# Expert gates formed from fp32r matmuls of 256 columns a token, in 64 blocks of four tokens

## The reference, cut to what matters

```
s1 = einsum('thd,kd->thk', q[..., :half], keys1);  v1, i1 = top_k(s1, 16)
s2 = einsum('thd,kd->thk', q[..., half:], keys2);  v2, i2 = top_k(s2, 16)
expert = i1 * 128 + i2          # of the 16 best of the 16x16 sums
gate   = softmax(top_s)
z   = einsum('cd,ced->ce', xc, u[expert])
act = gelu(z) * gate
y   = einsum('ce,ced->cd', act, v[expert])
```

## Time and profile before

| | |
|---|---|
| median of three timed runs | 2793.49 us |
| the profiled execution | 2792.25 us, span 2790.4 us |
| PE busy | 2752.2 us (99%) |
| PEld busy | 2406.8 us (86%) |
| DVE busy | 1807.2 us (65%) |
| ACT busy | 1391.5 us (50%) |
| POOL busy | 281.9 us (10%) |
| HBM read | 501.49 MB, 184 GB/s over the span |

### The profile page before, as it was taken

The page is one execution under the profiler, slowest core; times in us unless marked ns, Lnnn a source line. Parts: engine busy times, 40 slices in busy tenths (PEclk is TensorE's granted clock), DMA queues, the critical chain, the costliest instruction groups (busy, mean ns, idle before and its releaser), DMA issues.

```text
span 2790.4 us, 49534 instructions
## 1 busy us (share of the span) xinstructions
PE 2752.2 (99%) x15456; PEld 2406.8 (86%) x15456; DVE 1807.2 (65%) x2899; ACT 1391.5 (50%) x2037; POOL 281.9 (10%) x390
## 2 busy tenths in 40 slices
PE   8999999999999999999999999999999999999998
PEld 6888878888888888889998999888888888888887
DVE  6666665658986666478886666666665555555555
ACT  5454545556665444455555554555454444444444
POOL 0000000000001110000005996000000000000000
PEclk9999999999999999999999999999999999999999
DMA  6544445564555444555565444666666555555564
GB/s 250 188 152 165 156 162 188 180 214 163 173 174 162 155 156 143 193 186 184 186 211 165 156 160 158 217 212 211 213 207 195 193 192 194 193 192 194 192 236 159
DMA packets 153554, 514.76 MB, mean 184 GB/s; under 512 B 17056, under 2 KB 33696, under 8 KB 152480
## 3 DMA queue, kind: packets, MB, share of 16 engines
q1 hardware_dynamic: 131904, 480.44, 52.1%
q10 hardware_dynamic: 21600, 33.70, 3.4%
HBM read 501.49 MB, written 12.58 MB: 184 GB/s over the span
## 4 chain that ended last, share of the span: by engine, by line
PE 86%; issue 10%; DVE 2%; POOL 1%; ACT 1%; DMA 1%; POOLq 0%; DVEq 0%; ACTq 0%; SPq 0%
PE bank L504 21%; PE bank L509 11%; PE bank L2215 8%; PE bank L2217 8%; PE bank L2216 8%; PE bank L542 4%; PE bank L543 4%; PE bank L544 4%; PE bank L489 4%; PE bank L490 4%; PE bank L491 4%; PE bank L2190 2%; DVE w_lo L466 1%; DMA raw<-in_stream 1%; POOL big L623 0%
## 5 line engine op out<-in xcount | busy, mean ns | idle before, releaser
L466 DVE TENSOR_TENSOR w_lo<-raw,w_hi 128x1024 fp32r<-128x1024 f32 x904 | 1096.6, 1224 | 800.8 <-ACT w_hi L457 795.4
L457 ACT ACTIVATE w_hi<-raw 128x1024 fp32r<-128x1024 f32 x904 | 953.2, 1059 | 982.1 <-PE bank L2217 370.1
L504 PE MATMUL bank<-act,w_hi 128*128 128x512 f32 x3072 | 787.0, 398 | 1.1 <-DVE big L1261 1.1
L504 PEld LDWEIGHTS bank<-act,w_hi 128*128 128x128 f32 x3072 | 554.5, 189 | 106.4 <-issue 4.8
L509 PEld LDWEIGHTS bank<-act,w_lo 128*128 128x128 f32 x3072 | 418.7, 190 | 31.0
L509 PE MATMUL bank<-act,w_lo 128*128 128x256 f32 x3072 | 427.9, 282 | 0.0
L2215 PE MATMUL bank<-w_hi,expert_act 128*128 128x512 f32 x1008 | 392.4, 389 | 0.2
L2217 PE MATMUL bank<-w_hi,expert_act 128*128 128x512 f32 x1008 | 392.1, 389 | 0.0
L2216 PE MATMUL bank<-w_lo,expert_act 128*128 128x512 f32 x1008 | 392.1, 389 | 0.0
L489 PE MATMUL bank<-act,w_hi 128*128 128x256 f32 x912 | 260.8, 286 | 3.3 <-DVE w_lo L466 2.7
L491 PE MATMUL bank<-act,w_lo 128*128 128x256 f32 x912 | 258.6, 284 | 0.0
(11 more groups left out here) (307 smaller groups left out, 2553.2 us busy)
## 6 DMA issues: line engine op xcount, KB each, us to landing
raw<-in_stream SPq DMA_DIRECT2D x904, 512.0 KB, 4.2
big<-in_ukv ACTq DMA_DIRECT2D x16, 512.0 KB, 4.5
z_kept<-cst ACTq DMA_DIRECT2D x64, 128.0 KB, 3.2
cst<-z_kept ACTq DMA_DIRECT2D x64, 128.0 KB, 3.9
big<-in_x SPq DMA_DIRECT2D x2, 1024.0 KB, 8.2
big<-in_rows ACTq DMA_DIRECT2D x2, 1024.0 KB, 9.5
big<-in_rg_w ACTq DMA_DIRECT2D x1, 2048.0 KB, 11.8
x_kept<-big ACTq DMA_DIRECT2D x1, 2048.0 KB, 6.8
```

What stands on the lines that cost most here:

```text
L457: act.activation(w_hi[:, s, :], raw[:, s, :], ACT.Copy).then_inc(hi_ready, 1)
L466: dve.tensor_tensor(w_lo[:, s, :], raw[:, s, :], w_hi[:, s, :].bitcast(F32), ALU.subtract).then_inc(lo_ready, 1)
L504: pe.matmul(bank[:, :], w_hi[:, s, kk * P:(kk + 1) * P], act2[:, k, :, :].rearrange("p a n -> p (a n)"), start=(k == 0), stop=False)
```

## The change

The gates go to fp32r. ACT makes `gate_hi`, DVE `gate_lo`. For each token one DVE instruction (scalar_tensor_tensor, 256 elements) writes both weighted one-hot halves into `weighted`, POOL writes the 0/1 matrix in fp32r, and one PE matmul of 256 columns gives the token's high and low gates side by side in PSUM. ACT copies the low half into G and DVE adds the high half from PSUM.

A block now has four tokens instead of eight, so the stage `u_gates` has 64 blocks instead of 32, and `u_late` has 32 instead of 64. The four matmuls run between the wide and the narrow matmuls of the pair's second unit, after one set of waits for all four. Of the 96 z now stored, 32 come back in `u_late` and 64 in the first 32 turns of the stage `v`.

```diff
@@ sizes, storage
-         ("wqu", 4 * PH), ("u_decode", 2 * PH), ("u_gates", S // 8), ("u_late", NB // 2), ("v", NB)]
-EARLY = NB // 2
+         ("wqu", 4 * PH), ("u_decode", 2 * PH), ("u_gates", S // 4), ("u_late", NB // 4), ("v", NB)]
+EARLY = 3 * NB // 4
+LATE = NB - EARLY
...
-        hot = sb("hot", [P, 2, 4, P])
+        weighted = sb("weighted", [P, 4, 2, P], F32R)
+        GATE_BANKS = [[banks[0], banks[1]], [banks[4], banks[5]]]
@@ halves_out
+                if u and between:
+                    between()
                 pe.wait_ge(lo_ready, 2 * pair + u + 1)
@@ scalar
+            act.activation(gate_hi.bitcast(F32R), gate_lo, ACT.Copy).then_inc(slots_kept, 1)
-            with act.Fori(0, S // 16) as i:
+            with act.Fori(0, S // 8) as i:
                 for n in range(2):
...
-                    ahead(split_hi, act, "u_gates", i, 2, n, units=(0,))
-                    keep_gates(0)
-                    ahead(split_hi, act, "u_gates", i, 2, n, units=(1,))
+                    for u in range(2):
+                        ahead(split_hi, act, "u_gates", i, 2, n, units=(u,))
                     act.wait_ge(unit_done, 2 * pair_of("u_gates", i, 2, n) + 2)
                     act.wait_ge(z_saved[n], i * 16 + (32 * PH + 1))
                     low_half(act, GZ[:, n, :], banks[2 + n])
-                    keep_gates(1)
+                    for half in range(2):
+                        act.wait_ge(hot_used[2 * half + 1], i * 2 + n + 2)
+                        act.activation(G[:, :, bass.ds(i * 8 + (4 * n + 2 * half), 2)],
+                                       GATE_BANKS[n][half].rearrange("p (t a b) -> p a b t", t=2, a=2)[:, 1, :, :],
+                                       ACT.Copy).then_inc(gate_low, 1)
                     wait_summed(act, block_of("u_gates", i, 2, n))
                     act.activation(GZ[:, n, :], GZ[:, n, :], ACT.Gelu).then_inc(gelu_ready[n], 1)
...
+            with act.Fori(0, (EARLY - LATE) // 2) as i:
+                for n in range(2):
+                    act.wait_ge(early_ready[n], i + (LATE // 2 + 1))
+                    act.dma_start(GB[:, n, :], z_kept[bass.ds(i * 2 + (LATE + n), 1), :, :]
+                                  .rearrange("o p n -> (o p) n")).then_inc(z_back[n], 16)
+                next_experts(i)
@@ vector
+            step(dve.tensor_tensor(gate_lo, gate_lo, gate_hi, ALU.subtract))
+            step.wait()
+            def add_gates(i, n):
+                for half in range(2):
+                    dve.wait_ge(gate_low, i * 4 + (2 * n + half + 1))
+                    dest = G[:, :, bass.ds(i * 8 + (4 * n + 2 * half), 2)]
+                    high = GATE_BANKS[n][half].rearrange("p (t a b) -> p a b t", t=2, a=2)[:, 0, :, :]
+                    dve.tensor_tensor(dest, dest, high, ALU.add).then_inc(gate_kept[n], 1)
+            with dve.Fori(0, S // 8) as i:
                 for n in range(2):
-                    for s in range(8):
...
+                    for s in range(4):
+                        tok = i * 8 + (4 * n + s)
+                        dve.wait_ge(hot_used[s], i * 2 + n + 1)
+                        dve.scalar_tensor_tensor(
+                            out=weighted[:, s, :, :], in0=iota.unsqueeze(1).broadcast_to([P, 2, P]),
+                            scalar=first_index[:, bass.ds(tok, 1)],
+                            in1=slot_t[:, 1:3, bass.ds(tok, 1)].broadcast_to([P, 2, P]),
+                            op0=ALU.is_equal, op1=ALU.mult).then_inc(hot1, 1)
+                        if s == 1 and n == 1:
+                            add_gates(i, 0)
+                        if s % 2:
+                            ahead(split_lo, dve, "u_gates", i, 2, n, units=(s // 2,))
                     add_halves(dve, GZ[:, n, :], banks[2 + n], block_of("u_gates", i, 2, n))
+                add_gates(i, 1)
...
+            with dve.Fori(0, (EARLY - LATE) // 2) as i:
                 for n in range(2):
+                    next_expert(i, n)
+                    dve.wait_ge(z_back[n], i * 16 + (8 * LATE + 16))
+                    back = G[:, bass.ds(i * 2 + (LATE + n), 1), :].rearrange("p o n -> p (o n)")
+                    dve.tensor_tensor(back, GB[:, n, :], back, ALU.mult).then_inc(early_ready[n], 1)
@@ tensor
+            def four_tokens(i, n):
+                pe.wait_ge(gate_kept[n], i * 2 + 1)
+                pe.wait_ge(hot1, i * 8 + (4 * n + 4))
+                pe.wait_ge(hot2, i * 8 + (4 * n + 4 + 1))
+                for s in range(4):
+                    pe.matmul(GATE_BANKS[n][s // 2][:, (s % 2) * S:(s % 2 + 1) * S], hot[:, s, :],
+                              weighted[:, s, :, :].rearrange("p a b -> p (a b)"), start=True, stop=True)\
+                      .then_inc(hot_used[s], 1)
+            with pe.Fori(0, S // 8) as i:
                 for n in range(2):
                     pe.wait_ge(gelu_ready[n], i + (2 * PH + 1))
...
+                    halves_out(pe, pair_of("u_gates", i, 2, n), n, banks[2 + n], between=lambda: four_tokens(i, n))
```

More of the change, by code:

```diff
@@ L83 @@
 _n = 0
-for _name, _count in [("conv", 4 * CONV_J), ("rnn", 2 * KT), ("heads", 2 * H2), ("u_gates", S // 8),
-                      ("u_late", NB // 2)]:
+for _name, _count in [("conv", 4 * CONV_J), ("rnn", 2 * KT), ("heads", 2 * H2), ("u_gates", S // 4),
+                      ("u_late", LATE)]:
     HALVED[_name] = _n
@@ L162, in build @@
             pass
-        hot = sb("hot", [P, 2, 4, P])
+        weighted = sb("weighted", [P, 4, 2, P], F32R)
+        with nc.sbuf_tensor("below_hot", [P, CONST["causal"][0]], F32), \
+                nc.sbuf_tensor("hot", [P, 4, P], F32R) as hot:
+            pass
         cst = sb("cst", [P, CONST_W])
@@ L268, in build @@
         G = big[:, :].rearrange("p (b t) -> p b t", b=NB)
+        first_index = slot_t[:, 0, :]
+        second_index = par[:, 0:S]
+        gate_hi = slot_t[:, 1, :]
+        gate_lo = slot_t[:, 2, :]
+        GATE_BANKS = [[banks[0], banks[1]], [banks[4], banks[5]]]
         GZ = c("band").rearrange("p (s n) -> p s n", s=2)
@@ L426, in build @@
         hot_used = [sem(f"hot_used{n}") for n in range(4)]
+        gate_low = sem("gate_low")
         gate_kept = [sem(f"gate_kept{n}") for n in range(2)]
@@ L495, in block_of, with halves_out @@
             return i * per + (HALVED[part] + k)
-        def halves_out(pe, pair, odd, bank, units=(0, 1)):
+        def halves_out(pe, pair, odd, bank, units=(0, 1), between=None):
             for u in units:
@@ L628, in _ @@
                 pool.wait_ge(hot2, i * 8 + 1)
-                pool.tensor_copy(idx8, slot_t[:, 1, bass.ds(i * 8, 8)]).then_inc(g_step, 1)
+                pool.tensor_copy(idx8, second_index[:, bass.ds(i * 8, 8)]).then_inc(g_step, 1)
                 pool.wait_ge(g_step, i + 1)
@@ L1005, in _ @@
                 act.wait_ge(picks_turned, 2 * a + 2)
-                act.activation(slot_t[:, a, :], banks[4 + a][:, 0:S], ACT.Copy).then_inc(slots_kept, 1)
+                act.activation([first_index, second_index, gate_lo][a], banks[4 + a][:, 0:S], ACT.Copy).then_inc(slots_kept, 1)
             act.wait_ge(slots_kept, 3)
             act.wait_ge(x_saved, 16)
-            with act.Fori(0, S // 16) as i:
+            act.activation(gate_hi.bitcast(F32R), gate_lo, ACT.Copy).then_inc(slots_kept, 1)
+            with act.Fori(0, S // 8) as i:
                 for n in range(2):
[L1012 to L1016, removed]
-                    ahead(split_hi, act, "u_gates", i, 2, n, units=(0,))
-                    keep_gates(0)
-                    ahead(split_hi, act, "u_gates", i, 2, n, units=(1,))
+                    for u in range(2):
+                        ahead(split_hi, act, "u_gates", i, 2, n, units=(u,))
                     act.wait_ge(unit_done, 2 * pair_of("u_gates", i, 2, n) + 2)
@@ L1049, in expert_hi @@
                 act.activation(expert_hi_t[:, n, :], G[:, bass.ds(b, 1), :].rearrange("p o n -> p (o n)"), ACT.Copy)                   .then_inc(eh_ready, 1)
-            with act.Fori(0, EARLY // 2 - 1) as i:
+            with act.Fori(0, LATE // 2 - 1) as i:
                 late_turn(i)
@@ L1055, in _ @@
                 expert_hi(n, n, 2 * FIRST["u_late"])
-            late_turn(EARLY // 2 - 1)
+            late_turn(LATE // 2 - 1)
             for n in range(2):
-                act.wait_ge(act_ready[n], EARLY // 2 + 1)
-                act.wait_ge(early_ready[n], EARLY // 2 + 1)
+                act.wait_ge(act_ready[n], LATE // 2 + 1)
+                act.wait_ge(early_ready[n], LATE // 2 + 1)
             def next_experts(i):
@@ L1063, in next_experts @@
                     expert_hi(i * 2 + (2 + n), n, 2 * pair_of("v", i, 2, n) + 2)
-            with act.Fori(0, NB // 2 - 8) as i:
+            with act.Fori(0, (EARLY - LATE) // 2) as i:
[4 more added lines that the diff above has]
+                next_experts(i)
+            for n in range(2):
+                act.wait_ge(early_ready[n], EARLY // 2 + 1)
```

(47 more changed lines are left out.)

2 lines of the change are left out of this document (1 added, 1 removed).

## The result

The changed kernel takes 3017.28 us (3015.96 to 3020.77, four runs) against 2792.84 us (2789.01 to 2794.49): the ratio is 1.0809, 95% interval 1.0797 to 1.0822. The forecast was 2958 us with a range of 2910 to 3050 us. Its chain of waits is there step by step; the 59 us that it missed are a lower clock of TensorE (65 us, against 6 to 9 us by which the chain is shorter than forecast), which it had as a rival and left out of its sum.

The account below looks back on a forecast made before the run. PE, busy for 99% of the span, was taken as the bound. 64 x 9.19 + 32 x 5.545 = 765.6 us against 600.7 us, 165 us more, gave 2958 us, range 2910 to 3050 us.

Parts of the forecast that it names:

- The wait and who causes it: In u_gates, PE waits before the tokens for DVE's one-hots 2 and 3, behind w_lo of unit 0: 3.1 us idle a block.
- The chain to the tokens: In u_gates, from ACT's w_hi of the last block's unit 1 until PE starts the tokens: 7.32 us.
- From the tokens to ACT's next `w_hi`: In u_gates, 12 matmuls at 0.12 us, ACT's hand-over and 0.10 us for filling an empty array: 1.87 us together.
- fp32r tokens: In u_gates, four token matmuls of 256 columns on PE cost 0.48 us in place of 0.95 us.
- What is hidden: Gate additions, tokens 0 and 1, ACT's copies and POOL's one-hots in u_gates, and the z returning in v, add 0 us.
- The clock: TensorE's clock in u_gates stands at 1.00 despite a gap near 3 us a block; its fall was left to a rival.
- a mix: The clock in u_gates falls and recovers in part, ending between 2958 and 3150 us; within a rival of chance 14%.
- the second rival: The clock falls in u_gates' gaps: 12.2 us a block, 192 us more, 3150 us if it never recovers; chance 14%.
- The argument against the clock's fall: Two thirds of each u_gates block are dense matmuls; the 3.29 us gap that lost the clock followed small matmuls and transposes.
- the signs that it named: In u_gates: PE busy near two thirds, idle about 3 us before tokens, blocks 9.2 us, token pitch 0.12 us, clock 1.00.
- the upper bound: Top of the total's range, 3050 us, for a clock that falls in some of the gaps.

Follow-up runs that it names:

- the two fillings: Changed kernel plus 12 or 6 useless wide matmuls a block ahead of the four tokens: 2952.26 us with 12, 2952.10 us with 6.
- the kernel with ACT's new order: Changed kernel, but ACT makes w_hi of the next block's unit 0 ahead of Gelu and the z store: 2887.70 us.
- the kernel where nothing waits: Changed kernel with both edits: DVE writes four one-hots ahead of both w_lo splits, PE multiplies tokens after unit 1's narrow matmuls: 2761.34 us.
- the filling's run: Changed kernel plus 12 useless wide matmuls of 512 columns a block, ahead of the four tokens: 2952.26 us.
- the kernel with single waits: Changed kernel, but PE waits for each of the four tokens by itself instead of once for all four: 2962.27 us.
- DVE's move alone: Changed kernel, but DVE writes all four one-hots ahead of both w_lo splits; PE's place stays: 2795.41 us.
- PE's alone: Changed kernel, but PE's four tokens come after unit 1's narrow matmuls and unit_done; DVE's order stays: 2816.96 us.

## Why the prediction was right, and where it was short

- **The wait and who causes it: right.** PE waits ahead of the tokens for DVE's `weighted`, 63 times; tokens 2 and 3 stand behind `w_lo` of unit 0. Undoing either half of the arrangement takes away 200 to 222 us of the loss, the clock's part included.
- **The chain to the tokens: right in each term.** 7.32 us was forecast as the mean of the two kinds of block; 7.48 and 7.16 us are measured. Its terms there are 1.18, 1.15, 0.44, 1.39 (loop turns), 1.17, 1.15 and 1.00 us, the last with the wake. Without a fallen clock the block is 9.05 us (the two fillings) against 9.19.
- **From the tokens to ACT's next `w_hi`: too long by 0.14 us.** The forecast had 1.87 us, of it 0.10 us for filling an empty array, a term that no row stood for. In the kernel with ACT's new order PE starts the tokens after a gap at full clock at 1702.61 and ACT follows at 1704.34: 1.73 us, which leaves no such term to see.
- **fp32r tokens: right.** 0.48 us for four in the kernel where nothing waits, and 0.95 us before.
- **What is hidden: right.** Two strided gate additions take 0.78 us together, where one `add_halves` takes 0.41 us, and `v` costs nothing more.
- **The clock: the step that was short.** The forecast took "the clock stands at 1.00" as the likely case, because an idle of 1.98 us had left it there. The case "a mix" of the second rival is what happened: the clock fell in or behind 57 of the 63 gaps, mostly for about 3.5 us, and not in six of 1.52 to 1.58 us. The term is 10.1 - 9.05 = 1.05 us a block, 65 us by the filling's run. The full price of the rival, 3.0 us a block, was three times too high, because unit 0's narrow matmuls and unit 1 run at full clock again.
- **The argument against the clock's fall: misread.** The forecast set the gap at 354 us apart because it came "after small matmuls and transposes". Only 16 transposes stood between it and dense matmuls of the kind that `u_gates` has. In the kernel before:

```profile
350.49 1.12 PE L509 MATMUL bank<-act,w_lo 128*128 128x256 f32 x8
351.44 1.90 PE L1938 MATMUL bank<-big 128*128 x16
```

- **The signs and the range.** Of the signs that it named, the clock at 1.00, blocks of 9.2 us and a busy share of PE near two thirds (it is 488.32 of 638.79 us, 0.76) didn't come. The four tokens take 1.22 us in the block shown and 0.74 us at full clock, near the slow pitch that it had named as a sign of being wrong. That 3017 us still lies inside the range is in part luck: the upper bound, 92 us above the forecast, was set for a clock that falls in some of the gaps at 3.0 us each, some 31 of them. It fell in nearly all, at a third of the price.
- The Trainium skill ("TensorE: Matmul & The Clock Gate", "Why this matters for your kernels") warns of idle gaps of some microseconds between bursts of matmuls. The trace agrees in kind: in the changed kernel the clock fell in or behind each gap of 1.83 to 2.89 us. The rival should have had more than 14%.

What stays open is what decides whether the clock falls. In the kernel with single waits a gap of 2.37 us leaves it at 1.00 and one of 1.47 us is followed by 0.50 (timeline rows, then windows with the same columns as above):

```profile
1731.67 0.78 PE L2231 MATMUL bank<-weighted,hot 128*128 128x256 f32 x2 [2.37 <-DVE weighted L1782]
1824.75 0.78 PE L2231 MATMUL bank<-weighted,hot 128*128 128x256 f32 x2 [1.47 <-DVE weighted L1782]
...
1733.00:1734.00 1.00, 1.00 (x8) 0.87 (x7) 0.00 (x0) 0.56 (x1) 0.63 (x2) 1.00 0.81 324
1827.00:1828.00 1.00, 1.00 (x4) 0.81 (x3) 0.15 (x1) 1.00 (x3) 0.00 (x0) 0.50 0.00 0
```

And the gap of 1.98 us on which the forecast rested stands, with the same work before it, in every kernel here. In the kernel with both edits the clock is at 0.50 behind it:

```profile
1104.31 1.74 PE L2141 MATMUL bank<-big 128*128 128x256 f32 x4 [1.98 <-ACT big L959]
...
1105.00:1106.00 1.00, 1.00 (x4) 0.82 (x3) 0.00 (x0) 0.20 (x1) 0.00 (x0) 0.50 0.43 172
```

It fell there in four of the ten profiled executions and stayed in six. So the length of a gap alone doesn't decide, and one gap that left the clock up was too little to make "it stands at 1.00" the likely case.

## What to carry to other kernels

When an instruction is moved earlier on one engine, follow each thing that it waits for back through the written order of the producer's queue: here a cheap one-hot stood behind a split that needed PE's own last unit, and the loop closed through five engine hand-overs. The producer must be moved with the consumer: DVE's move alone gave back all but 4 us of the loss, PE's alone all but 25 us, and only both gave the gain of 1.1%. One gap in one trace that left the clock up doesn't show that the next one will. If a stall of 2 to 3 us in a block can't be avoided, price it with TensorE's lower clock behind it, and wait for pieces one by one rather than for the last.

## What the runs showed of the hardware that was not expected

The clock was lowered by idle gaps that took only about a quarter of each block, among dense matmuls, and 768 matmuls whose result nobody reads bought 65 us by keeping it up; half of them did the same. The same gap of 1.98 us, with the same work around it, lowered it in four of ten executions, and within one kernel a gap of 1.47 us lowered it and one of 2.37 us didn't.
